# Second feed-forward matmul of a hybrid decoder block as seven block products, with the weight sums made in DRAM by adding DMAs

## The reference

```
h = rms_norm(x, g_ffn_norm[l])
x = x + jnp.square(jax.nn.relu(h @ w_ff1[l])) @ w_ff2[l]
```

## Time and profile before

| | us |
|---|---|
| median of three runs | 634.78 (633.72 to 634.92) |
| the profiled execution, its own time | 633.49 |
| its span, first to last instruction | 631.8 |
| PE busy | 617.6 (98% of the span) |
| DVE, ACT, POOL busy | 325.5, 264.6, 11.0 |
| share of PE on the chain that ended last | 91% |
| mean DMA rate | 95 GB/s |

### The profile page before, as it was taken

The page is one execution under the profiler, slowest core; times in us unless marked ns, Lnnn a source line. Parts: engine busy times, 40 slices in busy tenths (PEclk is TensorE's granted clock), DMA queues, the critical chain, the costliest instruction groups (busy, mean ns, idle before and its releaser), DMA issues.

```text
span 631.8 us, 8695 instructions
## 1 busy us (share of the span) xinstructions
PE 617.6 (98%) x3130; PEld 515.5 (82%) x3130; DVE 325.5 (52%) x577; ACT 264.6 (42%) x503; POOL 11.0 (2%) x31
## 2 busy tenths in 40 slices
PE   7999999999999999999999999999999999999997
PEld 5888677788898888988888888888888888888885
DVE  5699981686688686564333333334433333333323
ACT  7656552737466656462222222223333333222220
POOL 1400000000000000000000000000000000000000
PEclk9999999999999999999999999999999999999999
DMA  8512447342121020004223322332222323322003
GB/s 341 181 42 66 134 137 262 102 167 67 34 68 67 0 68 1 1 1 139 95 99 100 100 100 100 100 98 94 87 89 100 100 100 100 100 100 97 36 0 134
DMA packets 17228, 60.08 MB, mean 95 GB/s; under 512 B 2144, under 2 KB 2432, under 8 KB 17200
## 3 DMA queue, kind: packets, MB, share of 16 engines
q1 hardware_dynamic: 16416, 57.88, 27.0%
q0 software_dynamic: 640, 1.82, 0.9%
q10 hardware_dynamic: 144, 0.01, 0.0%
HBM read 57.60 MB, written 2.10 MB: 94 GB/s over the span
## 4 chain that ended last, share of the span: by engine, by line
PE 91%; DVE 4%; ACT 2%; issue 1%; POOL 0%; DVEq 0%; ACTq 0%; POOLq 0%
PE ps L317 26%; PE ps L319 25%; PE ps L318 25%; PE ps L1687 4%; PE ps L1675 2%; PE ps L1636 1%; PE ps L1422 1%; PE ps L1545 1%; PE ps L1637 1%; DVE ht_lo L955 1%; PE ps L1508 1%; PE ps L1617 1%; DVE w_lo_sb L933 1%; ACT ht_hi L564 1%; PE ps L1597 1%
## 5 line engine op out<-in xcount | busy, mean ns | idle before, releaser
L317 PE MATMUL ps<-ht_hi,w_hi_sb 128*128 128x512 f32 (+1 forms) x280 | 107.7, 385 | 0.0
L319 PE MATMUL ps<-ht_hi,w_lo_sb 128*128 128x512 f32 (+1 forms) x280 | 107.3, 383 | 0.0
L318 PE MATMUL ps<-ht_lo,w_hi_sb 128*128 128x512 f32 (+1 forms) x280 | 107.3, 383 | 0.0
L317 PE MATMUL ps<-w_hi_sb,a_hi 128*128 128x512 f32 x256 | 99.6, 389 | 0.0
L318 PE MATMUL ps<-w_lo_sb,a_hi 128*128 128x512 f32 x256 | 99.6, 389 | 0.0
L319 PE MATMUL ps<-w_hi_sb,a_lo 128*128 128x512 f32 x256 | 99.6, 389 | 0.0
L317 PE MATMUL ps<-w_hi_sb,ht_hi 128*128 128x512 f32 x192 | 82.1, 427 | 3.0 <-DVE ht_lo L955 1.6
L1293 DVE TENSOR_TENSOR w_lo_sb<-raw,w_hi_sb 128x1024 fp32r<-128x1024 f32 x64 | 78.3, 1225 | 10.2 <-ACT w_hi_sb L809 5.0
L319 PE MATMUL ps<-w_hi_sb,ht_lo 128*128 128x512 f32 x192 | 75.3, 392 | 0.0
L318 PE MATMUL ps<-w_lo_sb,ht_hi 128*128 128x512 f32 x192 | 75.1, 391 | 0.0
L1358 DVE TENSOR_TENSOR act_sb<-act_sb (+1 forms) x32 | 22.2, 692 | 102.8 <-ACT act_sb L891 102.8
(11 more groups left out here) (189 smaller groups left out, 791.0 us busy)
## 6 DMA issues: line engine op xcount, KB each, us to landing
raw<-in_w_ff SPq DMA_DIRECT2D x64, 512.0 KB, 3.4
raw<-in_w SPq DMA_DIRECT2D x24, 512.0 KB, 4.6
xs<-in_x SPq DMA_DIRECT2D x8, 512.0 KB, 6.7
raw<-in_cmp_w SPq DMA_DIRECT2D x8, 512.0 KB, 4.7
out_y<-xs SPq DMA_DIRECT2D x3, 512.0 KB, 2.7
raw<-in_w_c SPq DMA_DIRECT2D x4, 304.0 KB, 2.8
spw_sb<-in_sp_w POOLq DMA_DIRECT2D x1, 512.0 KB, 3.6
grow_ffn<-in_g_ffn POOLq DMA_DIRECT2D x1, 512.0 KB, 3.8
```

What stands on the lines that cost most here:

```text
L317: pe.matmul(out, l_hi, r_hi, start=start, stop=False)
L318: pe.matmul(out, l_hi, r_lo, start=False, stop=False)
L319: return pe.matmul(out, l_lo, r_hi, start=False, stop=stop)
```

## The change

Both dimensions of the second product are halved. A is cut into row halves (256 rows) and halves of the 4096 (16 blocks of 128 each, HF = 16), W into the matching four blocks W11, W12, W21, W22 (512 columns wide). The host lays `w_ff2` out so, and `w_ff1` so that the hidden blocks k and k+16 come one after the other. Seven block products P1 to P7 take the place of eight. For each of the 16 block pairs k there are two steps on PE: one in group 1 (P1, P5, P6, P4: 4 x 2 x 3 = 24 matmuls) and, after all 16 of these, one in group 2 (P3, P2, P7: 18 matmuls).

The sums of A (S1 to S4) are made by DVE in SBUF (`sums`, `fourth_sum`), in a tensor `aq` that takes the place of `act_sb`. The sums of W are made in DRAM, in a new tensor `forms` with five blocks of 128x512 (256 KB) for each k: W11, W12+W11, that plus W22, that plus W21, and W12+W22. For each k POOL starts seven DMAs, one after another, each waiting for the one before it: a copy of two blocks, a copy of two blocks, three adding DMAs of one block, a copy of one block, an adding DMA of one block. Two such chains, for even and odd k, run side by side. They begin when the last row tile of the first feed-forward matmul's left operand is there (`ht_done`). A step of group 1 loads four blocks of `forms` (2 x 512 KB), and SP first waits until the seven DMAs of its k are done (`form_made`); a step of group 2 loads two blocks of `w_ff2` and the fifth of `forms` (512 + 256 KB).

Between the groups ACT and DVE combine the sums of P1, P5, P6, P4 out of PSUM into `part`, in three instructions that PE waits for (`p1_kept`, `kept`), and during the next steps DVE adds them with the residual into `xs` (`base`). The tail adds P7, P3 and P2 (`result`).

```diff
+HF = NF // 2
+TH = SEQ // 2
+U0 = NW + NF
+A11, S1, A22, S2, A12, A21 = range(6)
+S4, S3 = S2, A21
+FIRST = slice(A11, S2 + 1)
+SECOND = slice(S4, S3 + 1)
+
+PRODUCTS = {"P1": (A11, 0, 0, 0), "P5": (S1, 0, 1, 2), "P6": (S2, 1, 0, 4), "P4": (A22, 1, 1, 6),
+            "P3": (S4, 0, 0, 2), "P2": (A12, 0, 1, 0), "P7": (S3, 1, 0, 4)}
+G1, G1_LAST = ["P1", "P5", "P6", "P4"], ["P1", "P6", "P5", "P4"]
+G2, G2_FIRST = ["P3", "P2", "P7"], ["P2", "P3", "P7"]
+LAST_TWO = [("P7", 0, 0), ("P7", 1, 0), ("P3", 0, 0), ("P3", 1, 0), ("P7", 0, 1), ("P7", 1, 1), ("P2", 0, 0),
+            ("P3", 0, 1), ("P3", 1, 1), ("P2", 1, 0), ("P2", 0, 1), ("P2", 1, 1)]
...
+        a_hi = [at("a_hi0", [P, 4, TH], F32R, o_wh + SPARE * UW * 4), at("a_hi1", [P, 4, TH], F32R, o_ht[0])]
+        a_lo = [at("a_lo0", [P, 4, TH], F32R, o_wh + (SPARE + 1) * UW * 4), at("a_lo1", [P, 4, TH], F32R, o_ht[0] + 4096)]
+        nr2 = at("nr2", [P, 2], F32, o_ht[1] + 12288)
+        part = at("part", [P, 2, 3, 512], F32, o_ht[1])
 
 
         par = at("par", [P, 2, NKV, SEQ // 2], F32, o_x)
...
-            sp.wait_ge(y_out, 16 * (NT - 1 + len(LAST_COLS)))
+
+            def first_group(j, i):
+
+                J = i * 2 + j
+                for unit in range(2):
+                    sp.wait_ge(w_lo, J * 2 + (NS + NF - RAW + 1 + unit))
+                    sp.dma_start(raw[:, 2 * j + unit, :].rearrange("p (h n) -> p h n", h=2),
+                                 forms[J, 2 * unit:2 * unit + 2].rearrange("h p n -> p h n")
+                                 ).then_inc(raw_in[2 * j + unit], 16)
+
+            def second_group(j, i):
+
+                k, J = i * 2 + j, i * 2 + (HF + j)
+                sp.wait_ge(w_lo, J * 2 + (NS + NF - RAW + 1))
+                sp.dma_start(raw[:, 2 * j, :].rearrange("p (h n) -> p h n", h=2),
...
+            for i in range(HF // 2):
+                for j in range(2):
+                    sp.wait_ge(form_made[j], 16 * 7 * (i + 1))
+                    first_group(j, i)
+            with sp.Fori(0, HF // 2) as i:
+                for j in range(2):
...
+
+            def form_step(k, n):
+
+                out, src, op = [(slice(0, 2), w_ff2[k, 0:2], None), (slice(2, 4), w_ff2[k, 2:4], None),
+                                (1, w_ff2[k, 0], ALU.add), (2, forms[k, 1], ALU.add), (3, forms[k, 2], ALU.add),
+                                (4, w_ff2[k, 1], None), (4, w_ff2[k, 2], ALU.add)][n]
+                how = {} if op is None else {"accum_op": op, "max_dma_last_dim": 8192}
+                pool.dma_start(forms[k, out], src, **how).then_inc(form_made[k % 2], 16)
+
+            pool.wait_ge(ht_done, len(HT))
+            for i in range(HF // 2):
+                for n in range(7):
+                    for j in range(2):
+                        if i or n:
+                            pool.wait_ge(form_made[j], 16 * (7 * i + n))
+                        form_step(2 * i + j, n)
+
...
 
                 i, j = f
+                J = i * 2 + j // 2
                 act.wait_ge(w_used, i * FR + (NW + j + 1))
-                act.activation(act_sb[:, i * FR + j, :], ps[:, 4 + j, :], ACT.Relu).then_inc(bank_free, 1)
+                if j % 2 == 0:
+                    last = act.activation(aq[:, J, A11:A21 + 1:A21 - A11, :],
+                                          ps[:, 4 + j, :].rearrange("p (h n) -> p h n", h=2), ACT.Relu)
+                else:
+                    act.activation(aq[:, J, A12, :], ps[:, 4 + j, 0:TH], ACT.Relu)
+                    last = act.activation(aq[:, J, A22, :], ps[:, 4 + j, TH:], ACT.Relu)
+                last.then_inc(bank_free, 1)
...
+            def a_high(slot, k, pieces, used, sums):
+
+                act.wait_ge(w_used, used)
+                act.wait_ge(summed, sums)
+                n = pieces.stop - pieces.start
+                act.activation(a_hi[slot][:, 0:n, :], aq[:, k, pieces, :], ACT.Copy).then_inc(ah_done, 1)
...
+            def sums(i, j):
+
+                J, n = i * 2 + j // 2, i * 6 + 3 * (j // 2)
+                q = [aq[:, J, k, :] for k in range(6)]
+                dve.wait_ge(squared, i * FR + (j + 1))
+                dve.tensor_tensor(q[S1], q[A21], q[A22], ALU.subtract).then_inc(summed, 1)
+                dve.wait_ge(summed, n + 1)
+                dve.tensor_tensor(q[S3], q[A11], q[A21], ALU.subtract).then_inc(summed, 1)
+                dve.tensor_tensor(q[S2], q[S1], q[A11], ALU.subtract).then_inc(summed, 1)
+
...
+            def fourth_sum(k, count):
+
+                dve.wait_ge(al_done, count)
+                dve.tensor_tensor(aq[:, k, S4, :], aq[:, k, A12, :], aq[:, k, S2, :], ALU.add).then_inc(summed, 1)
...
+
+                form_lo(2 * j, J * 2 + (H0 + 1))
+                form_lo(2 * j + 1, J * 2 + (H0 + 2))
+                a_low(j, J, FIRST, J + 1)
+                fourth_sum(J, J + 1)
+
+            def second_group(j, i):
+
...
                     f_lo(j, i * FR + (2 * NS + FR + j + 1))
+                    if j % 2:
+                        sums(i, j)
             for j in range(FR):
                 square(NF // FR - 1, j)
...
+                    first_group(j, i * 2 + j)
+            second_group(0, 0)
+            dve.wait_ge(p1_kept, 1)
+            dve.wait_ge(p_whole, 2)
+            dve.tensor_tensor(part[:, :, 1, :], ps[:, 4:6, :], part[:, :, 0, :], ALU.add).then_inc(kept, 1)
+            dve.wait_ge(kept, 1)
+            dve.wait_ge(w_used, U0 + 2 * HF - 1)
+            dve.tensor_tensor(part[:, :, 2, :], ps[:, 2:4, :], part[:, :, 1, :], ALU.subtract).then_inc(kept, 1)
+            second_group(1, 0)
+            dve.wait_ge(w_used, U0 + 2 * HF)
+            dve.tensor_tensor(part[:, :, 1, :], part[:, :, 1, :], ps[:, 6:8, :], ALU.add).then_inc(kept, 1)
...
+            second_group(0, HF // 2 - 1)
+            i, J = HF // 2 - 1, 2 * HF - 1
+            form_lo(3, 2 * J + H0 + 1, 512)
+            a_low(1, HF - 1, SECOND, J + 1)
+            form_lo(2, 2 * J + H0 + 2)
+
+            def result(product, i, c=slice(0, 512)):
+
+                src = ps[:, PRODUCTS[product][3] + i, c]
+                if product == "P7":
+                    for rows, scale in ((xs[:, 2 + i, 0:512], stat(rstd, "ffn", 2 + i)), (xs[:, 2 + i, 512:], nr2[:, i:i + 1])):
...
+            def step(j, J, products, first=False, last=False):
+
+                units = [PRODUCTS[p][1] for p in products]
+                pe.wait_ge(al_done, J + 1)
+                for n, p in enumerate(products):
+                    unit = units[n]
+                    if unit not in units[:n]:
+                        pe.wait_ge(w_lo, J * 2 + (NS + NF + 1 + unit))
+                    if first and p == "P6":
                         pe.wait_ge(bank_free, NF)
-                    for b in range(2):
-                        mm = piece(j, t, slice(b * 512, b * 512 + 512), first, False)
-                mm.then_inc(w_used, 1)
-
-            for j in range(FR):
-                second(j, NS + NF + j + 1, j + 1, first=j == 0)
-            with pe.Fori(1, NF // FR - 1) as i:
-                for j in range(FR):
-                    second(j, i * FR + (NS + NF + j + 1), i * FR + (j + 1))
-            for j in range(FR - 2):
-                f = NF - FR + j
-                second(j, NS + NF + f + 1, f + 1)
-
-
-            for t, i in LAST_TWO:
-                j, f = FR - 2 + i, NF - 2 + i
-                if t == 0:
-                    pe.wait_ge(w_lo, NS + NF + f + 1)
-                    pe.wait_ge(al_done, f + 1)
-                for n in (slice(0, 512), slice(512, 1024)):
-                    mm = piece(j, t, n, False, i == 1)
-                    if i and t == NT - 1:
-                        mm.then_inc(m_done, 1)
-                if i and t < NT - 1:
+                    if first and p == "P2":
+                        pe.wait_ge(p1_kept, 1)
+                    if first and p == "P3":
+                        pe.wait_ge(kept, 2)
+                    if first and p == "P7":
+                        pe.wait_ge(kept, 1)
+                    for i in range(2):
+                        mm = piece(j, p, i, first, last)
+                    if unit not in units[n + 1:]:
+                        mm.then_inc(w_used, 1)
+                    elif last and p in ("P1", "P6"):
+                        mm.then_inc(p_whole, 1)
...
-        "w_ff2": i["w_ff2"][0].reshape(NF, P, D),
+        "w_ff1": i["w_ff1"][0].reshape(NK, P, 2, HF, P).transpose(3, 2, 1, 0, 4).reshape(NF, P, D),
+        "w_ff2": np.stack([w2[:HF, :, :512], w2[:HF, :, 512:], w2[HF:, :, 512:], w2[HF:, :, :512]], 1),
```

More of the change, by code:

```diff
@@ new lines, in _ @@
+                if j % 2:
+                    a_high(j // 2, j // 2, FIRST, NW + NF - (2, 0)[j // 2], 3 * (j // 2) + 3)
+            with act.Fori(1, HF // 2) as i:
+                for j in range(2):
+                    first_group(j, i)
+            second_group(0, 0)
+            act.wait_ge(p_whole, 1)
+            act.activation(part[:, :, 0, :], ps[:, 0:2, :], ACT.Copy).then_inc(p1_kept, 1)
```

(55 more changed lines are left out.)

167 lines of the change are left out of this document (103 added, 64 removed).

## The result

The changed kernel takes 676.63 us (674.89 to 678.77, 4 runs) against 634.66 before in the same series: ratio 1.0666, 95% interval 1.063 to 1.0702. It is 42 us slower. The forecast was 613.3 us, in a range of 611 to 656.

What follows compares the result with a forecast made beforehand. PE was taken as the only bound. Span 631.8 - 21.8 (96 matmuls) + 0.4 (seams) - 0.1 (end) = 610.3; with 1.7 around the span 612.0, and 1.3 for the median: 613.3 us, range 611 to 656.

Steps and rivals of the forecast that it cites:

- late chains: Rival: POOL's chains take 4.9 us a round, end 37 us late, PE waits in group 1; 650 us, chance 0.36.
- the term for a round: One DMA of each of POOL's two chains: 4.0 us, 56 rounds, chains end at 507, 14 us early.
- adding DMAs "3.7": POOL's adding DMAs of 256 KB: two passes through the engines, since a second operand is read, 3.7 us each.
- a copy of 256 KB, "2.93": POOL's one-block copy in each chain: fixed part 2.15 plus 0.78, 2.93 us.
- "a copy at the row": POOL's two 512 KB copies per chain: 3.7 us each, from loads started by POOL landing after 3.6 and 3.8.
- hand-off 0.1: Between one POOL DMA's landing and the next in its chain: 0.1 us a round.
- The twins are expected to take turns: The two chains' DMAs share a queue: the second is held back once, then stays behind; round 4.0 us.
- 0.3 for SP's loads: Added to each round of POOL's chains for the loads running beside them: 0.3 us.
- the upper bound: Round of POOL's chains if adding takes two passes and each DMA waits for its whole twin: 5.6 us, giving 690.
- the rule of the prediction: Chains must end by 521.0, so a round may take 4.25 us; each 0.1 over costs 5.6 us.
- The seams: Start of group 1 and passage between groups, where DVE work may hold PE: 0.4 us for both, bounds 0 and 4.
- Shapes and operand types are the same, so I keep the 0.2267: PE's matmul pitch stays 0.2267 us, so 96 fewer matmuls save 21.8 us.

Runs made afterwards that it cites:

- the placed version: The changed kernel with four chains side by side, plus 320 unused bytes in front of w_hi_sb: 612.55 us, ratio 0.9667.
- the version with copies: The changed kernel with the four adding DMAs of each chain as plain copies of the same rows and bytes: 627.98 us, ratio 0.9913.
- the version without chains: The changed kernel without POOL's weight-sum DMAs and the waits for them, SP loading plain blocks of w_ff2: 618.05 us, ratio 0.9759.

## Why the prediction was wrong

**The cause of the loss was in it, as the rival "late chains"; its chance and its price were too low.** The step that failed is the term for a round: "(2 x 3.7 + 2.93 + 4 x 3.7) / 7 + 0.4 = 4.0". It measured 5.3. Term by term:

- adding DMAs "3.7": 4.4 alone, 5.1 beside the twin. The 0.8 allowed for the adding was right for one chain (4.4 against 3.6 for the plain copy of the same bytes); what it was put on was too low.
- a copy of 256 KB, "2.93": 3.6, alone and beside the twin. The fixed part, 2.15, had been read from loads into SBUF; no row showed it for DRAM to DRAM.
- "a copy at the row" for 512 KB, 3.7: 4.4 alone on average (3.8 for the first of a pair, 4.9 for the second), 5.3 beside the twin.
- hand-off 0.1: 0.28. The earlier trace rows shows an ordinary POOL instruction going on at once after a landing, not a DMA being issued; this was a row of another kind.
- "The twins are expected to take turns": they do not. The twin costs 0.6 to 0.7 a round. This was the argument by which I chose 4.0 and not 4.9, and no row stood behind it.
- 0.3 for SP's loads: right. A round is 5.0 where SP loads little and 5.3 where it loads much, and 4.4 and 4.7 with one chain.

Together, where SP loads little: 4.0 - 0.3 = 3.7 was forecast for a chain alone and 4.4 was measured; the twin brings that to 5.0, and the loads to 5.3.

My "late chains" case had R = 4.9, and the upper bound 5.6. With 5.3 the rule of the prediction gives 56 x (5.3 - 4.25) = 59 us late, and 613 + 59 = 672; with the 5 us of the operands' places, 677. The mechanism was right; the numbers put into it were not, and the range was cut at R = 5.0 without a row for that. That 677 is so near 676.6 is in part luck. Group 1 began at 456.49 and not at 453.0, and its 14 steps took 5.53 on average, so step 14 was due at 534.0 and not at 529.2; but the even chain's last landing at 580.95 was 11.6 us ahead of that step's first matmul (592.54), not 8.2, and the chains began 2.2 us later than at 283.0. These shifts nearly cancel: the lateness of that step was 592.54 - 534.0 = 58.5.

**What was right.** The matmuls: the placed version has 5.44 us a step and starts its last matmul at 605.00; the sum had 626.88 - 21.8 + 0.4 = 605.5. The seams: no wait over 0.3 us at either, in the placed version. The slope behind the deadline: the version with copies had a round of 4.4, so the rule adds 56 x (4.4 - 4.25) = 8 us to the 618.0 of the version without chains; measured were 10. The traffic itself: with all DMAs, but in time, the kernel takes 618.6 and 617.9 us, without them 618.0. The last loads were dearer than taken: four at once, the chain that ended last shows 7.6 us for one, not 3.4.

**The total.** 677.0 - 615.7 (span of the version without chains) = 61.3 us. PE's holes, each from the start of one matmul to that of the next less a pitch, are 9.1 + 23.3 + 20.3 = 52.7, and the matmuls at the lower clock 8.4, in all 61.1. The clock was not in the prediction: I priced a hole at its length, and each also costs what PE is slower by behind it.

**What the forecast missed altogether.** "Shapes and operand types are the same, so I keep the 0.2267" failed in the changed kernel. The new allocation puts `w_hi_sb` behind the small tensors, at 320 modulo 512 bytes. Of the 21.8 us, about 6 were lost to this in every version whose operands start there: 4.3 in the two feed-forward matmuls and most of the 2.0 ahead of them. By the medians 320 or 64 unused bytes bring back 5 (617.86 to 612.55 and 613.07).

**The price of adding.** An adding DMA of 256 KB takes 0.80 us more of all engines than a plain copy of the same packets, where the earlier trace rows give 0.78 for the data part. The Trainium skill says in "Collectives: The Full Stack" (The bandwidth ceiling: the fold count), of a ring collective, that its adding half runs at half the rate of its copying half because the add reads two sources. The trace agrees: the data part doubles. To the landing the add costs more, 1.5 us beside the twin (5.1 against 3.6). The fit of "DMA: Bandwidth & Descriptors" (Anatomy of one DMA, SWDGE path) in the Trainium skill, 2.0 us + bytes / 436e3, gives 3.2 us for 512 KB and 2.6 for 256 KB. The plain copies from DRAM to DRAM had 5.3 and 3.6 beside the twin, and even alone 4.4 and 3.6.

**What stays open.** Of the 1.5 us of adding, 0.8 is engine time and some 0.3 the longer start on POOL; the last 0.4 has no row. How the twins hold each other up is open too: adding DMAs and copies of 512 KB suffer, the copy of 256 KB does not. That would fit a cost that goes with the engine time of a DMA, but no run here takes apart queue, engines, reading and writing. The starts modulo 128 are shown by four paddings; which of the two operands of a matmul matters more is only suggested by the even and odd steps (buffers at 320 and at 128, with the weights at 320: 5.49 and 5.60).

## What to carry to other kernels

A chain of DMAs in which each waits for the one before is priced by its landing times, not by bytes: 56 rounds of 5.3 us stood against 238 us of cover. Put more chains side by side while the DMA engines have idle time (four instead of two: a DMA in 1.7 us instead of 2.65, the engines' share from 0.82 to 1.00), or begin earlier, before making the DMAs cheaper. A row of a profile that mixes kinds of DMA has to be taken apart before it prices one of them. Where a deadline decides, state the sum as a function of the one unknown, and do not take the favourable value without a row for it. And a change of the SBUF allocation is a change of its own: look at the pitch of matmuls that were not meant to change.

## What the hardware showed that was not expected

- An adding DMA of 256 KB from DRAM to DRAM lands after 4.4 us alone (one run) and 5.1 beside a second chain; the plain copy after 3.6 in both cases. The add takes 0.80 us more of all 16 engines.
- A matmul of 128x512 in float32r with an operand that starts 64 bytes off a multiple of 128 has a pitch of 0.228 to 0.2333 us instead of 0.2267.
- Behind its three holes of 9 to 23 us PE works for a few microseconds at the lower clock level, which cost 8.4 us in all.
